# A two-block transformer kernel: mLSTM heads placed between the projection's products, and out products that end token tile by token tile

## The reference, cut to what matters

```python
def _mlstm_mixer(xn, w_in, b_gates, conv_w, head_g, w_out):
    proj = (xn @ w_in).astype(jnp.float32)          # 1024 -> 4*1024 + 16
    qk, v, o, gates = jnp.split(proj, [2 * 1024, 3 * 1024, 4 * 1024], axis=-1)
    qk = jax.nn.silu(_causal_depthwise_conv(qk, conv_w))   # 4 taps
    q, k = jnp.split(qk, 2, axis=-1)
    i_pre, f_pre = gates + b_gates                  # 8 and 8 columns
    hid = _mlstm(hd(q), hd(k), hd(v), i_pre, f_pre) # 8 heads of 128, 2 chunks of 128 tokens
    hid = hid * lax.rsqrt(jnp.mean(hid * hid, axis=-1, keepdims=True) + EPS)
    hid = hid * head_g.reshape(8, 128)
    hid = hid.reshape(bsz, t, 1024) * jax.nn.sigmoid(o)
    return hid @ w_out

# per head and chunk, in _mlstm:
p = einsum(qc, kc) * exp(dmat - m_t)                # scores times decay
h_num = einsum(p, vc) + w_inter * einsum(qc, c_prev)   # c_prev: state after chunk 0
hid = h_num / max(abs(n_num), exp(-m_t))

# around every mixer and feed-forward:
xn = _rms_norm(x, g[2]); x = x + _rms_norm(mixer(xn), g[3])
```

## Time and profile before

| what | value |
|---|---|
| time, median of 3 runs | 1711.91 us (1708.65 to 1720.69) |
| the profiled execution's own time | 1710.37 us |
| its span (first to last instruction) | 1708.6 us |
| PE busy | 1641.5 us, 96% |
| DVE busy | 976.2 us, 57% |
| ACT busy | 802.3 us, 47% |
| POOL busy | 51.1 us, 3% |
| DMA | 279.28 MB, mean 163 GB/s |

### The profile page before, as it was taken

One profiled execution on the slowest core, in us unless ns is written; L12 is line 12 of the kernel. 1 busy time (PEld: TensorE's weight loads), 2 busy tenths in 40 slices (PEclk: granted clock), 3 DMA queues, 4 the chain that ended last, 5 costly groups with the idle time before them and its releaser, 6 DMA issues.

```text
span 1708.6 us, 19530 instructions
## 1 busy us (share of the span) xinstructions
PE 1641.5 (96%) x7593; PEld 1338.0 (78%) x7593; DVE 976.2 (57%) x1224; ACT 802.3 (47%) x995; POOL 51.1 (3%) x93
## 2 busy tenths in 40 slices
PE   8999999889999999999878999999999999999999
PEld 6888777678888888878657888887777878777887
DVE  4554566465545645458535554566945565694555
ACT  5543555164435544354544444455445445535552
POOL 1000000000000000000000000001000000100000
PEclk9999999999999999989979999999999999999999
DMA  9644562145446553544502654554433546443343
GB/s 305 214 147 173 209 219 102 50 160 182 150 183 212 197 196 113 198 172 149 206 1 99 215 179 158 181 213 155 164 119 112 184 155 222 156 164 105 135 161 123
DMA packets 187061, 279.28 MB, mean 163 GB/s; under 512 B 8526, under 2 KB 98806, under 8 KB 186993
## 3 DMA queue, kind: packets, MB, share of 16 engines
q1 hardware_dynamic: 184720, 271.27, 45.6%
q0 software_dynamic: 2128, 7.04, 1.4%
q10 hardware_dynamic: 144, 0.03, 0.0%
HBM read 277.26 MB, written 1.06 MB: 163 GB/s over the span
## 4 chain that ended last, share of the span: by engine, by line
PE 80%; DVE 12%; ACT 4%; issue 2%; POOL 1%; DMA 0%; POOLq 0%; SPq 0%; ACTq 0%; DVEq 0%
PE ACC L656 21%; PE ACC L658 21%; PE ACC L657 21%; DVE WL L1698 5%; PE TB L687 2%; PE ZB L820 2%; ACT WH L1162 2%; PE ACC L853 2%; PE ACC L855 1%; PE ACC L854 1%; PE ACC L741 1%; PE ZB L823 1%; PE ACC L742 1%; PE ACC L743 1%; PE TB L675 1%
## 5 line engine op out<-in xcount | busy, mean ns | idle before, releaser
L1698 DVE TENSOR_TENSOR WL<-RAW,WH 128x2048 fp32r<-128x2048 f32 (+3 forms) x280 | 557.5, 2034 | 315.7 <-ACT WH L1162 312.4
L656 PE MATMUL ACC<-WL,XH 128*128 128x512 f32 (+2 forms) x1440 | 570.3, 396 | 12.1 <-issue 5.8
L658 PE MATMUL ACC<-WH,XL 128*128 128x512 f32 (+2 forms) x1440 | 561.1, 390 | 0.0
L657 PE MATMUL ACC<-WH,XH 128*128 128x512 f32 (+2 forms) x1440 | 560.6, 389 | 0.0
L1162 ACT ACTIVATE WH<-RAW 128x2048 fp32r<-128x2048 f32 (+3 forms) x280 | 463.4, 1705 | 180.0 <-PE ACC L658 110.3
L656 PEld LDWEIGHTS ACC<-WL,XH 128*128 128x128 f32 x1440 | 275.0, 191 | 73.1 <-issue 17.9
L658 PEld LDWEIGHTS ACC<-WH,XL 128*128 128x128 f32 x1440 | 274.7, 191 | 56.8
L657 PEld LDWEIGHTS ACC<-WH,XH 128*128 128x128 f32 x1440 | 275.4, 191 | 52.7
L656 PE MATMUL ACC<-WL,HH 128*128 128x512 f32 x352 | 138.2, 393 | 0.6
L658 PE MATMUL ACC<-WH,HL 128*128 128x512 f32 x352 | 137.1, 389 | 0.0
L657 PE MATMUL ACC<-WH,HH 128*128 128x512 f32 x352 | 137.0, 389 | 0.0
(11 more groups left out here) (257 smaller groups left out, 1553.8 us busy)
## 6 DMA issues: line engine op xcount, KB each, us to landing
RAW<-w_in_in SPq DMA_DIRECT2D x68, 1024.0 KB, 6.5
RAW<-ffn_w_gate_in SPq DMA_DIRECT2D x43, 1024.0 KB, 5.1
RAW<-ffn_w_up_in SPq DMA_DIRECT2D x43, 1024.0 KB, 7.4
RAW<-ffn_w_down_in SPq DMA_DIRECT2D x32, 512.0 KB, 4.5
RAW<-ffn_w_down_in SPq DMA_DIRECT2D x16, 1024.0 KB, 6.5
RAW<-mlstm_w_in_in SPq DMA_DIRECT2D x16, 1024.0 KB, 7.2
RAW<-ffn_w_down_in SPq DMA_DIRECT2D x16, 768.0 KB, 6.1
RAW<-attn_w_in_in SPq DMA_DIRECT2D x12, 1024.0 KB, 7.2
```

Of the source, the lines that this page charges most:

```text
L656: nc.tensor.matmul(bank, lh, wl[:, i, :], start=first and i == 0, stop=False)
L657: nc.tensor.matmul(bank, lh, wh[:, i, :], start=False, stop=False)
L658: mm = nc.tensor.matmul(bank, ll, wh[:, i, :], start=False, stop=last and i == k - 1)
L1698: nc.vector.tensor_tensor(WL[:, slot, lo:hi], RAW[:, slot, lo:hi], WH[:, slot, lo:hi].bitcast(F32), ALU.subtract).then_inc(lo_ready, 1)
```

## The change

1. mLSTM by a list. `mlstm_order` places all steps of the mLSTM stage at steps of the eight blocks, as `attn_order` does. The blocks run in the order q0, k0, v0, q1, k1, v1, o0, o1 (`MLSTM_COLS`), where 0 means heads 0 to 3 and 1 heads 4 to 7. Heads 0 to 3 have their scores in block 3 and their outputs from the end of block 3 into block 4, heads 4 to 7 in blocks 6 and 7. The banks of the scores and outputs are `ZB` and `OB`; the weighted scores are written into `XN` in place of `PT`. `MU` now has 128 partitions (rows 8 to 127 zero).
2. The convolution's first tap (shift 0) moves from DVE to ACT (`first_tap`, two ACTIVATE of 128x256 a group); the other three stay on DVE.
3. Norm, gating and mixing go by halves of four heads; k 0 to 3 of the out product read new buffers `MH` and `ML`, so part 0 follows block 7 directly, and the mixed groups 2 and 3 come inside it.
4. The out product of both mixers: part 1 goes half 0 tok 0, half 1 tok 0, half 0 tok 1, half 1 tok 1. The transposes of the next x stand ahead of the last two k, before ahead of the last. A semaphore `front_used` frees the first half of a weight slot after part 0 of half 0, and ACT and DVE split the next stage's first chunk in two pieces around the norm (`out_product`, `postnorm_by_token`).
5. In every stage's first block the transposes of tok 1 move from k = 4 to k = 6 (`product`).

```diff
...
-                order.append(("part", 1, n // KD, n // 4 % 2, 4 + n % 4))
+                order.append(("part", 1, n // 4 % 2, n // KD, 4 + n % 4))
...
+        MLSTM_COLS = (0, 2, 4, 1, 3, 5, 6, 7)
+        CONVOLVED = (0, 1, 4, 5, 2, 3, 6, 7)
+        def mlstm_order():
+
+            at_step, order = {}, []
+
+            def place(q, *step):
+                at_step.setdefault(q, []).append(step)
+
+            for j in range(8):
+                q = 2 * KD * j
+                if j:
+                    if j == 7:
+                        place(q, "evacuate", 6, 0)
+                    place(q, "evacuate", j - 1, 1)
+                place(q + 1, "hi", j + 1, 0)
+                if j - 1 in STAGED:
+                    n = 2 * STAGED.index(j - 1)
+                    place(q + 2, "staged", j - 1)
+                    place(q + 2, "tap", n)
+                    place(q + 4, "tap", n + 1)
+                    place(q + 5, "conv", n)
+                    place(q + 7, "silu", n)
+                    place(q + 10, "conv", n + 1)
+                    place(q + 13, "silu", n + 1)
+                place(q + 3, "hi", j + 1, 1)
+                place(q + 4, "lo", j + 1, 0)
+                place(q + 8, "lo", j + 1, 1)
+                if j != 6:
+                    place(q + 9, "evacuate", j, 0)
+            place(7, "sums")
+            place(9, "by_head")
+            place(14, "by_token")
+            place(15, "exps")
+            for half, q in ((0, 3 * 2 * KD), (1, 6 * 2 * KD)):
+                for i in range(4):
+                    h = 4 * half + i
+                    place(q + 1 + 2 * i, "scores", h)
+                    place(q + 2 + 2 * i, "decay", h)
+                    place(q + 3 + 2 * i, "weighted", h)
+                    place(q + 10 + 2 * i, "output", h)
+                    place(q + 11 + 2 * i, "taken", h)
+                    place(q + 12 + 2 * i, "added", h)
+                    place(q + 13 + 2 * i, "squared", h)
+                place(q + 4, "keys", half)
+                place(q + 7, "states", 2 * half)
+                place(q + 8, "states", 2 * half + 1)
+                place(q + 20, "normed", half)
+            q = 7 * 2 * KD
+            place(q + 3, "gated", 0)
+            place(q + 4, "scaled", 0)
+            place(q + 10, "mixed", 0)
+            place(q + 12, "mixed", 1)
+            for q in range(2 * KD * 8):
+                order += at_step.pop(q, [])
+                order.append(("mm", q // (2 * KD), q // KD % 2, q % KD))
+            for q in sorted(at_step):
+                order += at_step[q]
+            order += [("evacuate", 7, 1), ("hi", 9, 0), ("lo", 9, 0), ("hi", 9, 1), ("gated", 1), ("scaled", 1)]
+            for n in range(2 * KD):
+                if n == 11:
+                    order.append(("mixed", 2))
+                if n == 13:
+                    order += [("mixed", 3), ("lo", 9, 1)]
+                order.append(("part", 0, n // KD, n // 4 % 2, n % 4))
+            for n in range(2 * KD):
+                order.append(("part", 1, n // 4 % 2, n // KD, 4 + n % 4))
+            return order
+
...
-                for j in range(8):
+                for j in MLSTM_COLS:
...
+                        if fresh is not None and tok == 0 and i == k - 2:
+                            of_x(1, fresh + 2)
                         if fresh is not None and i in (0, k // 2):
-                            if tok == 0 and i:
-                                of_x(1, fresh + 2)
...
+                def first_tap(n):
+                    t = g0 + MLSTM_GROUP["staged", STAGED[n // 2], n % 2]
+                    act.wait_ge(groups_ready, t + 1)
+                    if n >= 2:
+                        act.wait_ge(silus, n - 1)
+                    for kk in range(2):
+                        i = 2 * CONVOLVED[n] + kk
+                        ins = nc.scalar.activation(YC[:, n % 2, kk * SEQ:(kk + 1) * SEQ], TB[t % 2][:, kk * SEQ:(kk + 1) * SEQ],
+                                                   ACT.Copy, scale=CW[:, i, 3:4])
+                    ins.then_inc(tapped, 1)
...
+            def out_product():
+                c = at.chunk + 2
+                at.front += 1
+
+                def next_hi(part):
+                    if part == 0:
+                        act.wait_ge(raw_ready[c % 2], raw_value(c))
+                    act.wait_ge(weights_used if part else front_used, c if part else at.front)
+                    cols = slice(part * SLOT // 2, (part + 1) * SLOT // 2)
+                    nc.scalar.activation(WH[:, c % 2, cols], RAW[:, c % 2, cols], ACT.Copy).then_inc(hi_ready, 1)
+
+                def out_square(half, tok):
+                    b = at.block + half
+                    if tok == 0:
+                        act.wait_ge(tile0_ready, b + 1)
+                    else:
+                        act.wait_ge(weights_used, at.chunk + half + 2)
+                    square(ACC[:, pair(b) + tok, :], ST[:, half, :], half * 2 + tok, 2)
+
+                next_hi(0)
+                out_square(0, 0)
+                out_square(1, 0)
+                out_square(0, 1)
+                x_hi(0, (0,))
+                next_hi(1)
+                x_hi(0, (1,))
+                out_square(1, 1)
+                at.chunk += 2
                 at.block += 2
-                postnorm(1)
+                at.rsqrt += 2
 
             def attn(layer, next_size):
...
+            def postnorm_by_token(between):
+
+                row = at.row % 2
+                dve.wait_ge(row_loaded[row], 16 * (at.row // 2 + 1))
+                at.row += 1
+
+                def scaled(half, tok):
+                    at.square += 1
+                    dve.wait_ge(squares, at.square)
+                    cols = slice(half * COLS, (half + 1) * COLS)
+                    return nc.vector.tensor_tensor(XN[:, tok, cols], ACC[:, pair(at.block - 2 + half) + tok, :], G[:, row, cols],
+                                                   ALU.mult)
+
+                def add(tok, half):
+                    cols = slice(half * COLS, (half + 1) * COLS)
+                    nc.vector.scalar_tensor_tensor(X[:, tok, cols], XN[:, tok, cols], RS[:, tok:tok + 1], X[:, tok, cols],
+                                                   ALU.mult, ALU.add).then_inc(x_ready, 1)
+
+                scaled(0, 0)
+                step(scaled(1, 0))
+                at.rsqrt += 1
+                dve.wait_ge(rsqrts, at.rsqrt)
+                add(0, 0)
+                add(0, 1)
+                scaled(0, 1).then_inc(blocks_used, 1)
+                x_lo(0, (0,))
+                between()
+                x_lo(0, (1,))
+                scaled(1, 1).then_inc(blocks_used, 1)
+                dve.wait_ge(blocks_used, at.block + 1)
+                at.rsqrt += 1
+                dve.wait_ge(rsqrts, at.rsqrt)
+                add(1, 0)
+                add(1, 1)
...
```

602 lines of the change are left out of this document (340 added, 262 removed).

## The result

The changed kernel takes **1689.31 us** (median of 4 runs, 1685.32 to 1694.56), the kernel before 1712.43 beside it; ratio 0.985, 95% interval 0.982 to 0.988. Timed again later it gave 0.986, interval 0.983 to 0.988. The forecast was 1691, the range 1678 to 1704. The profiled executions have spans of 1708.6 and 1683.5 us: 25.1 less, where the prediction's sum was 20.2.

A forecast was written before the change was run, and what follows sets the result against it. PE, busy 96% of the span, was taken to bound the kernel. Terms 21.4 - 2.6 + 7.0 - 5.6 gave 20.2 us gained, 1690.2 for the profiled execution, so 1691 us forecast; range 1678 to 1704.

The forecast's parts named there:

- A: mLSTM heads' stretch without product matmuls goes, its work returning between products: 21.4 us gained.
- B: mLSTM blocks: old PE stops go (+5.6 us), new ones from in-order queues come (-8.2): 2.6 us lost.
- five places named: New PE stops in mLSTM: block 2 0.65 us, block 3 1.25, block 5 2.55, block 6 0.8, block 7 1.3.
- in block 7 the gated heads come 1.3 late: mLSTM block 7: `mixed` 0 waits 1.3 us because DVE does gates, a low part, norm and eight products in a row.
- D: Tok 1's transposes two k later in every stage: 5.6 us lost, 1.36 in three stages and 0.75 in two.
- C: End of both out products: stops for X go and the next stage's block 2 starts earlier, 7.0 us gained.
- The rule on the shared port: GpSimd and DVE block each other, so tok 1's sum could wait up to 2.25 us for a low part.
- R1: Everything is covered, with no new stops and no cost from later transposes: 34 us gained, 1678; chance 0.12.
- R2: In-order queues stop PE 2.5 us with a clock dip in each of blocks 2 to 6: 1704; chance 0.23 with R4.
- R3: Small fp32 matmuls and short stops among the blocks keep PE at 1.2 GHz: slower, 1729; chance 0.05.
- R4: First scores of each half wait a whole half stage, halving the heads' gain: 9.5 us, 1702; chance 0.23 with R2.

The follow-up runs named there:

- experiment 6: Changed kernel with the scores, states and outputs of all eight mLSTM heads behind block 7 instead of between products; 0.989 of the kernel before.
- experiment 2: Kernel before the change with only tile 1's transposes moved from k = 4 to k = 6; 1.0024 of the kernel before.
- experiment 4: Changed kernel with block 7's weight splits for the first out-product chunk placed later on ACT and DVE; 0.982 of the kernel before.
- experiment 7: Changed kernel with the next stage's first weight split behind the squares and its low part behind tile 0's additions, after both out products; 0.990 of the kernel before.
- experiments 9 and 10: Changed kernel with tile 1's transposes at k = 6 only after the two mixers, elsewhere k = 4: 0.985; and the changed kernel unedited beside it: 0.986.

## Why the prediction came out right

**A, forecast 21.4, was 26.5.** The stretch did go: 44.7 + 1.6. The head work between products was mis-sized. I took a head round of 2.37 us plus two switches, 2.57; between products a head costs 1.34 + 0.69 = 2.03, eight of them 16.2 for 20.6. The round of before had no wait in it. It was longer by some 0.38 us at the rows around MU, whose form the change alters; I priced the new code by the old code's rows. The switches cost 0.04 more than the same rows take without products (1.32 in experiment 6, 0.67 in the kernel before), not 0.2. The k transposes take 0.45 a half and the states 0.9 (797.16 to 798.66 less a triple, and a switch): with two mixed groups 19.8 for 24.9. The 44.7 has before's slow clock in it, 4 to 6 us that experiment 2's trace doesn't have; forecast and measurement share it.

**B, forecast -2.6, was -5.1.** The old stops went (+5.6). Of five places named four have a stop, with the releaser that was named. One has the size, block 5 2.54 (2.55); two are a third smaller, block 2 0.46 (0.65) and block 3 0.86 (1.25); block 6 has none (0.8). The step that failed is "in block 7 the gated heads come 1.3 late": 3.65. I had counted DVE's low part and left out ACT, which copies the last head's output behind a table load, two gates and a split; in experiment 4 the split alone was 1.6 of the 3.8 us by which the norm came earlier. Behind that stop the clock fell a second time (0.72 from 866 to 872), 1.7 more; behind block 5 it fell as I had said (0.85 over 10.2 us, 1.5). 7.5 + 3.2 - 5.6 = 5.1.

The errors of A and B had opposite signs, and their sum 21.4 was forecast as 18.8. The total came out right partly by luck: two errors of 5.1 and 2.5 that cancel, a D that was too dear, and a trace of before with slow clock in it.

**C, forecast 7.0, was 7.4**, 3.1 behind attention (3.0) and 4.3 behind mLSTM (4.0), with each landmark of the chain within 0.1 us, the stop at k = 4 0.3 shorter. This is the term that was right step by step. The rule on the shared port would have made it 2.5. The trace does show the block: POOL's sum for tile 1 began beside DVE's low part at 899.19, took 0.62 us for the 0.19 of tile 0, and ended at 899.81, the low part at 899.77; in experiment 7, where more of the low part was left, it took 2.06. So the sum waited for the end of that instruction in each of these cases, and in the change 0.6 us of it were left where I had reckoned 0.3. It cost nothing, since the one that needs the root is DVE itself: the root was ready at 900.73, and DVE was busy with XL and the scaling until 901.40 (in experiment 7 907.21 and 907.88). The Trainium skill, "Advanced Engine Details and Errata", section "VectorE Performance Modes", says it only of those DVE instructions that use two ports, and its table gives the low part's kind, tensor_tensor, no such mode; these rows show the wait for it all the same.

**D, forecast -5.6, was -3.4 (the table) to -4.3 (experiments 9 and 10).** The steps in attention and the fourth stage were 1.38 and 1.40, as reckoned (1.36). The first stage pays 0.2 to 1.4, the second block's first 1.0, its second nothing that can be told from the clock.

**The rivals.** R1 is out: there are four new stops in the mLSTM stage. R2's five stops of 2.5 with slow clock became two. R3: clock 0.95 and 0.96 in the stretches, 1.00 between 787 and 808 us, where the scores and outputs stand. By the Trainium skill, "TensorE: Matmul & The Clock Gate", section "A second HAM failure mode: psum-queue depth-cycling", small idles could have swung it; for the heads' matmuls of 128x128 to 128x256 the trace doesn't agree. In the blocks it fell behind the stops of 2.54 and 3.65 us. But it was at 0.50 from 738 to 750 us too, before and after the change alike, in the stage's small block: 128x16 matmuls, in the change behind a stop of 1.31 and one of 0.35. Half of what the first stretch lacks to 1.00 lies there, so these traces don't clear small work in general. R4 is out: the first scores of the two halves waited 0.86 us and not at all.

## What to carry to other kernels

Price work that goes between products by its own rows, and look first whether the change alters their form: here a matmul operand that went from 8 to 128 partitions came with 0.38 us less a head. Follow a wait back past the engine that it is put down to, to where that engine stood idle itself: in in-order queues the late piece can be a weight split that nobody needs yet, and moving it a few steps, on ACT and on DVE, gave 5.0 us here. And look at every place that a shared helper serves: the later transposes cost 4 us in the stages that had no use for them.
